# Sparse attention: the queries' root mean squares as scale of the exponential instead of a normalisation of the queries

## The reference, cut to what matters

```python
def rms_norm_2(x, g):
    y = xf * lax.rsqrt(jnp.mean(xf * xf, axis=-1, keepdims=True) + EPS)
    return (y * g.astype(jnp.float32)).astype(x.dtype)

q = rms_norm_2((c_q @ w_qb).reshape(b, s, DSA_HEADS, DSA_HEAD_DIM), q_norm_g)
kv = c_kv @ w_kvb
k = rms_norm_2(kv[..., :DSA_HEAD_DIM], k_norm_g)
...
logits = jnp.einsum("bqhd,bqkd->bqhk", q_b, k_sel) * (DSA_HEAD_DIM ** -0.5)
logits = jnp.where(valid[:, :, None, :], logits, -jnp.inf)
p = jax.nn.softmax(logits, axis=-1)
return jnp.einsum("bqhk,bqkd->bqhd", p, v_sel)
```

## Time and profile before

| | us |
|---|---|
| median of three runs | 961.83 (961.36 to 965.58) |
| the profiled execution | 961.84, of which 960.0 are the span of the profile |
| PE busy | 877.3 (91% of the span) |
| weight loads busy | 774.2 |
| DVE busy | 577.4 |
| ACT busy | 408.6 |
| POOL busy | 137.1 |
| mean granted clock of TensorE | 0.963 of full speed |

### The profile page before, as it was taken

The page is one execution under the profiler, slowest core; times in us unless marked ns, Lnnn a source line. Parts: engine busy times, 40 slices in busy tenths (PEclk is TensorE's granted clock), DMA queues, the critical chain, the costliest instruction groups (busy, mean ns, idle before and its releaser), DMA issues.

```text
span 960.0 us, 13518 instructions
## 1 busy us (share of the span) xinstructions
PE 877.3 (91%) x5610; PEld 774.2 (81%) x5610; DVE 577.4 (60%) x831; ACT 408.6 (43%) x555; POOL 137.1 (14%) x176
## 2 busy tenths in 40 slices
PE   6987998998999999999859978879988889999998
PEld 5985976897899999999548777578767679999996
DVE  4349673536468777766618997666263657555552
ACT  4367233444336544443324553523143445444440
POOL 0150000210100000000207895053000000000000
PEclk9996998998999999999979899899998999999999
DMA  8964344353256565564043423002023138665541
GB/s 286 298 193 140 129 156 152 111 192 115 88 197 217 181 209 185 175 200 152 0 135 119 144 88 132 1 1 89 1 88 124 52 129 267 190 199 182 175 132 44
DMA packets 92344, 136.01 MB, mean 142 GB/s; under 512 B 4435, under 2 KB 76763, under 8 KB 92028
## 3 DMA queue, kind: packets, MB, share of 16 engines
q1 hardware_dynamic: 90428, 129.90, 41.4%
q10 hardware_dynamic: 1120, 2.62, 0.8%
q0 software_dynamic: 736, 2.63, 0.8%
HBM read 133.56 MB, written 1.06 MB: 140 GB/s over the span
## 4 chain that ended last, share of the span: by engine, by line
PE 76%; DVE 14%; ACT 4%; issue 3%; POOL 2%; DMA 2%; SPq 0%; POOLq 0%; DVEq 0%; ACTq 0%
PE work L2042 32%; PE acc L2042 25%; PE work L2497 3%; PE work L1998 3%; DVE split_extra_slot L1379 1%; DVE split_operands L1379 1%; PE work L2019 1%; DMA weight_ring<-in_w_in 1%; DVE arena L1658 1%; ACT hT L906 1%; PE work L2316 1%; PE work L1987 1%; PE work L2296 1%; PE work L2194 1%; PE work L2004 1%
## 5 line engine op out<-in xcount | busy, mean ns | idle before, releaser
L2042 PE MATMUL work<-split_operands 128*128 128x256 f32 x1824 | 223.9, 283 | 4.0 <-DVE split_operands L1379 4.0
L2042 PEld LDWEIGHTS work<-split_operands 128*128 128x128 f32 x1824 | 221.7, 192 | 6.1 <-issue 5.0
L1379 DVE TENSOR_TENSOR split_operands<-weight_ring,split_operands 128x2048 fp32r<-128x2048 f32 x73 | 167.8, 2302 | 94.3 <-ACT split_operands L926 93.8
L2042 PE MATMUL acc<-split_operands 128*128 128x512 f32 x840 | 197.6, 391 | 3.5 <-DVE split_operands L1541 2.5
L2042 PEld LDWEIGHTS acc<-split_operands 128*128 128x128 f32 x840 | 155.9, 188 | 36.4 <-DVE split_operands L1541 2.9
L926 ACT ACTIVATE split_operands<-weight_ring 128x2048 fp32r<-128x2048 f32 x73 | 139.1, 1910 | 103.4 <-PE acc L2042 45.9
L2042 PE MATMUL work<-split_operands,split_extra_slot 128*128 128x256 f32 x1056 | 137.7, 292 | 17.3 <-DVE split_extra_slot L1379 14.7
L2042 PEld LDWEIGHTS work<-split_operands,split_extra_slot 128*128 128x128 f32 x1056 | 135.1, 200 | 19.9 <-issue 16.3
L1379 DVE TENSOR_TENSOR split_extra_slot<-weight_ring,split_extra_slot 128x2048 fp32r<-128x2048 f32 x34 | 78.5, 2310 | 50.8 <-ACT split_extra_slot L926 50.5
L913 ACT ACTIVATE arena<-work 128x512 f32<-128x512 f32 (+1 forms) x68 | 37.6, 559 | 147.0 <-PE work L2042 86.7
L926 ACT ACTIVATE split_extra_slot<-weight_ring 128x2048 fp32r<-128x2048 f32 x34 | 64.9, 1909 | 57.4 <-DMA weight_ring<-in_w_in 19.9
(11 more groups left out here) (310 smaller groups left out, 937.8 us busy)
## 6 DMA issues: line engine op xcount, KB each, us to landing
weight_ring<-in_mlp_w SPq DMA_DIRECT2D x32, 1024.0 KB, 5.5
weight_ring<-in_w_up SPq DMA_DIRECT2D x22, 1024.0 KB, 5.1
weight_ring<-in_w_in SPq DMA_DIRECT2D x20, 1024.0 KB, 6.5
weight_ring<-in_w_down SPq DMA_DIRECT2D x11, 1024.0 KB, 4.8
weight_ring<-in_w_out SPq DMA_DIRECT2D x8, 1024.0 KB, 4.8
weight_ring<-in_w_mk SPq DMA_DIRECT2D x4, 1024.0 KB, 6.2
weight_ring<-in_w_mv SPq DMA_DIRECT2D x4, 1024.0 KB, 5.4
weight_ring<-in_w_mq SPq DMA_DIRECT2D x4, 1024.0 KB, 4.9
```

Source lines behind the costliest of these rows:

```text
L1379: dve.tensor_tensor(slot[:, 1, :], weights(split_units[i], 2048), slot[:, 0, :], ALU.subtract).then_inc(low_ready, 1)
L2042: ins = pe.matmul(out, lhs(p), rhs(q), start=(start and n == 0), stop=(stop and n == 2))
```

## The change: what it does

The sum of squares is made with the squares as the stationary operand, in four small matmuls of two columns (columns 63 and 64 of the block matrix): the result is [128 tokens, 8], one column for each token tile and head. Root and reciprocal work on that 128x8 tile. `dqT` keeps the raw queries. The query's weights are multiplied to the keys by one more `tensor_scalar`. The maximum of the raw logits is multiplied by the inverse root per token and head (`dve.tensor_tensor` on 128x2 for each of the four `dl` tiles), and ACT takes the exponential with the negative inverse root as its scale operand, one value per partition, where it was the constant -1. The first of the two reductions of a tile is now waited for on DVE by its own semaphore (`link`), and `d_max` is raised by the new multiplication, not by the first reduction.

```diff
+        dq_root, dq_neg_root = [cut(3992 + 8 * i, TT, DSA_HEADS) for i in range(2)]
@@ across_root, ACT
-                src = bank(name)[:, 0:SEQ] if tag == "dk" else halves(name)
-                act.activation(sq, src, ACT.Sqrt, scale=scale, bias=eps_col(bias)).then_inc(reader(name), 1)
+                roots = sq if tag == "dk" else dq_root.rearrange("p t h -> p (t h)")
+                src = bank(name)[:, 0:SEQ if tag == "dk" else TT * DSA_HEADS]
+                act.activation(roots, src, ACT.Sqrt, scale=scale, bias=eps_col(bias)).then_inc(reader(name), 1)
@@ exponentials, ACT
-                        ins = act.activation(dprobs[t][:, h, :], dprobs[t][:, h, :], ACT.Exp, scale=-1.0,
-                                             bias=dsoft[:, t, 0, h:h + 1],
+                        ins = act.activation(dprobs[t][:, h, :], dprobs[t][:, h, :], ACT.Exp,
+                                             scale=dq_neg_root[:, t, h:h + 1], bias=dsoft[:, t, 0, h:h + 1],
                                              accum_out=dsoft[:, t, 1, h:h + 1])
@@ across_norm, DVE
-                link(dve.reciprocal(sq, sq))
-                if gain is None:
-                    ins = dve.tensor_tensor(raw, raw, sq, ALU.mult)
+                if tag == "dq":
+                    link(dve.reciprocal(dq_root, dq_root))
+                    ins = dve.tensor_scalar(dq_neg_root, dq_root, -1.0, None, ALU.mult)
                 else:
-                    ins = dve.scalar_tensor_tensor(out=raw, in0=raw, scalar=parc(gain), in1=sq, op0=ALU.mult, op1=ALU.mult)
+                    link(dve.reciprocal(sq, sq))
+                    link(dve.scalar_tensor_tensor(out=raw, in0=raw, scalar=parc(gain), in1=sq, op0=ALU.mult, op1=ALU.mult))
+                    ins = dve.tensor_scalar(raw, raw, parc("dq_norm"), None, ALU.mult)
@@ maximum of the logits, DVE
                         if j == 0:
-                            ins.then_inc(d_max, 1)
+                            link(ins)
                     ins.then_inc(reader(name), 1)
+                    dve.wait_ge(*drained(name))
+                    low = dsoft[:, t, 0, :].rearrange("p (j e) -> p e j", e=2)[:, par, :]
+                    dve.tensor_tensor(low, low, dq_root[:, t, :].rearrange("p (j e) -> p e j", e=2)[:, par, :], ALU.mult
+                                      ).then_inc(d_max, 1)
@@ across_sum, PE
-                    ones = conc("block_ones") if tag == "dq" else conc("ones")
-                    ins = pe.matmul(ps[:, :], ones, sq.rearrange("p c t -> p (c t)"), start=True, stop=True)
+                    for t in range(TT):
+                        for c in range(2):
+                            at = DSA_HEADS * t + 2 * c
+                            ins = pe.matmul(ps[:, at:at + 2], sq[:, c, P * t:P * t + P], conc("block_ones")[:, DK - 1:DK + 1],
+                                            start=True, stop=True)
```

## The result

The changed kernel takes 965.94 us (median of 20 runs, 964.06 to 967.07) beside 962.46 us of the kernel before (20 runs, 960.68 to 966.77): ratio 1.0032, 95% interval 1.0022 to 1.0041. The medians lie 3.5 us apart, and by the ratio the change costs 3.1 us; 961.8 was forecast, with a range to 964.6. The profiled execution has a span of 962.6 us, 2.6 more than before.

A forecast was written before the change was run, and what follows sets the result against it. PE held the chain for three quarters of the span, with DVE setting the end at 544 to 583 us and ACT at the exponentials. 961.84 us, less 1.0, plus 0.95, gave 961.8; range 958.4 to 964.6.

The forecast's parts named there:

- What bounds the kernel: PE mostly; the edit counts where DVE sets the end, 544.74 to 583.43 us, and at ACT's exponentials from 609.28.
- DVE's own saving: Roots, reciprocals and key weights on DVE: 4.02 us removed, 0.79 added, 3.2 gained; bounds 3.0 to 3.4.
- How much arrives: At DVE's low part of `qkv` 3, held by ACT's copy: 0.6 + 0.4 = 1.0 us gained; bounds 0.6 to 3.2.
- Second stretch: Maxima and exponentials before DVE's division: ACT starts 0.2 us later, exponentials take 0.74 more; 0.95 us lost, bounds 0.7 to 1.3.
- The sum at the division: At DVE's division near 612.2 us: 1.0 us gained earlier against 0.95 lost, so about as before.
- The sum: Whole kernel: 961.84 us, less 1.0, plus 0.95, gives 961.8; 960.8 to 962.6 got a chance of 0.45.
- rival (b): Saving does not pass ACT's copy: 962.5 us, or 963.9 with the clock low under one more unit; chance 0.2.
- a clock that falls in the long levels of the gated rule behind: Example of something unseen, of either sign, behind the two changed places; no size given, chance 0.1.
- Rival (a): Clock rises sooner under `qkv` 1, so the saving arrives more fully: 960.1 us, or 959.6 in full; chance 0.25.
- the first stretch: DVE work from the queries' root reciprocal at 544.74 us to the low part of `z` 0: 1.0 us gained.

The follow-up runs named there:

- a_after: The changed kernel run again unaltered, for a second trace on another occasion: 965.76 us, 1.0035 against the kernel before.
- c: The changed kernel with three idle matmuls of 512 columns in PE's wait before the last row broadcast: 963.67 us, 1.0017.
- r: The kernel before with the convolution norm's variance moved ahead of the row sums, idle matmuls before the column transposes and in four later PE waits: 959.32 us, 0.9963.
- n: The changed kernel with one idle matmul in each of four PE waits from the cross attention to the MLP: 964.62 us, 1.0021.
- i: The changed kernel with the variance of the convolution's norm moved ahead of the row sums: 963.49 us, 1.0007.
- h: The kernel before with the variance of the convolution's norm moved ahead of the row sums: 963.87 us, 1.0010.
- p: The changed kernel with idle matmuls before the last row broadcast and in four waits from cross attention to MLP: 963.48 us, 1.0013.
- q: The kernel before with idle matmuls before the last row broadcast and in four waits from cross attention to MLP: 962.93 us, 1.0003.
- o: The changed kernel with the convolution norm's variance moved ahead of the row sums, idle matmuls before the column transposes and in four later PE waits: 959.08 us, 0.9969.
- f: The kernel before with only the change's small roots, reciprocals and key weights; exponential scale and early signal stay as before: 965.88 us, 1.0032.
- g: The kernel before with only the exponential's scale read from a column of -1, linked reductions and maxima multiplied by ones: 966.1 us, 1.0032.
- j: The kernel before with one useless DVE product of 0.7 us before the first maximum of the cross attention: 962.37 us, 1.0012.
- l: The changed kernel with three useless DVE products, planned at 2.8 us, before the first maximum of the cross attention: 964.09 us, 1.0016.

## Why the prediction was wrong, point by point

- **What bounds the kernel, DVE from 544 to 583 us, ACT at the exponentials**: right. Both stretches answer as described.
- **DVE's own saving, 3.2 us**: the new forms took 0.18, 0.22 and 0.35 us for the estimated 0.20, 0.16 and 0.35, and the index sums start 3.2 us earlier (550.89 to 546.85, less 0.76, is 3.28). Right.
- **How much arrives, 1.0 us, held up by ACT's copy of `qkv` 3**: the low part started 0.85 us earlier, with 1.14 us of idle time in front. The roots gave the 0.4 us that was counted. By the convolution's mean it is 1.2 us, because the low part itself fell from 2.83 to 2.29 us. Right.
- **Second stretch, 0.95 us**: the exponentials grew by 94 ns at 128x256 (492 to 586) and 92 at 128x128 (390 to 482), 0.74 us in all. The Trainium skill, page "ScalarE: Activation LUTs", section "What ACT_TABLE_LOAD costs", has about 93 ns for an operand given by a pointer; the trace agrees. ACT starts 0.63 us behind the first reduction, not 0.73. The second reduction starts 0.25 us behind the first, where it was 0.16, so the link costs 0.09 us. The page "VectorE: DVE Perf Modes" of the Trainium skill, section "The DRAIN you can't avoid", measured no cost for it on a chain of copies, and by that the link would be free; the trace of these reductions says otherwise.
- **The sum at the division, 0.05 us gained**: 0.03 in the first trace, 0.9 lost in the second (a_after), where the clock was low under `z` 0. The costs were right, and what they come to at this point hangs on the clock already.
- **The step that failed** is the one from there to the end: "The sum. 961.84 us [...], less 1.0, plus 0.95: 961.8". It took all that follows the division as a block that only moves. In the trace this block grew by 3.4 us net: 1.7 lost behind the exponentials, 1.1 gained ahead of the cross attention, 2.8 lost at the logits of the cross attention and the first unit of the MLP, each at a place at which PE waits and the granted clock then falls or does not. I had written of a moved wait that lets the clock go low, but only as an addition to rival (b), for one unit of 1.4 us (963.9), and had left 0.1 for "a clock that falls in the long levels of the gated rule behind". In the changed kernel it did not fall there but in the stages with short waits, and at several of them; in c and r it fell in the gated rule too and cost 1.5 us each. Besides, the sum started from a median of three runs, 961.83; that of 20 is 962.46, so that 0.6 of the 4.1 us between forecast and result lie there.
- **Rival (a)**, that the clock rises sooner under `qkv` 1, did not come in the first trace: 7.90 us after 7.72. In the second it did, 6.59 us, and the low part of `qkv` 3 started 1.7 us earlier than before; but the clock then fell under `z` 0, which took 7.47 us, and nothing of it was left at the division. In the first trace the slow unit of 7.4 us moved from `qkv` 5 to `qkv` 4, where PE waits for DVE behind it, and cost nothing.
- **Rival (b)** had the right sign, 0.7 to 2.1 us up, by a cause that was only partly right: the saving of the first stretch did pass ACT's copy.

What the runs show of the cause: it is the clock. The stages that take longer are PE's, with the lower clock in their windows, and c gives back 2.1 us of the median and n 1.1 with matmuls that compute nothing. Where the clock's falls lie otherwise, the change's cost does not show (i beside h -0.4 us, p beside q 0.55, o beside r -0.2, against 3.5), though no pair alone excludes a cost of 1 us. And the loss does not come through work added: f, with less work than the kernel before, loses as much as g, with more. That it comes through the shift of the later stages is what fits; the two runs that were to show it by a delay, j and l, do not, since DVE's waits took most of the delay. What stays open is the rule by which a wait of 1.56 us is harmless at one moment and costs 1.4 us at another. The traces fit with moments that are set early in the run. In 12 of the 17 traces read, the distance from the fall of the clock near 73 us to the gate rows at 525 us lies between 452.2 and 452.6 us, whatever was changed behind. In the other five it differs, and in two of them, a and p, it is 451.7 us: these are the two in which `qkv` 1 takes 6.6 us and `z` 0 7.47, while `qkv` 1 takes 7.90 to 7.98 in all other traces with the first half of the change. No run here sets that moment, so this was not tested. Nor is it shown why c lost 2.6 us at 628.

## What to carry to other kernels

When the direct costs of an edit cancel, forecast a spread and not a zero: list every place behind the edit where PE waits a microsecond or more on the chain, with the granted clock of the rows behind it, since a shift of less than a microsecond can turn each of them from full to half clock. A low stretch of the clock is a loss only where PE is on the chain; look for what DVE does beside it first. And before judging a small saving, fill PE's waits with idle matmuls in both kernels: here a saving of 2.4 us was invisible without them (963.87 and 963.49 beside 962.47 us), and with them the two kernels came to 959.32 and 959.08. Filling some of the waits is not enough: q's trace lost 1.5 us in one that was left (10.16 for 8.69 us).

## What was not expected of the hardware

- Two halves of a change cost 3.4 and 3.6 us alone and 3.5 together (965.88, 966.1 and 965.94 against 962.46 us): times near a clock that falls and rises are not additive.
- The same 32 matmuls of the first MLP unit, behind the same wait of PE (1.55 to 1.56 us), took 7.14 us in the kernel before and in l, 8.56 in the changed kernel and 10.19 in h.
- Two executions of the changed kernel had the clock low under different units ahead of the division, which moved it by 0.9 us.
- A wait on DVE's own semaphore between two reductions costs 0.09 us; an exponential with one more operand per partition 0.093 us.
